# Seven block products in place of eight in the second input projection of a two-block sequence model

## The chip, the cores and the metric

The program runs on one core of one Trainium2 chip, as one launch. Time is the device time of that core in microseconds; the median of three runs counts, and another execution was taken by the hardware profiler.

The engines are named as in the profile: PE (TensorE, matrix multiply; PEld is its weight load), DVE (VectorE), ACT (ScalarE), POOL (GpSimd) and SP (SyncE), which here issues all the DMAs. SPq rows are DMAs being issued by SP.

## The reference

Two blocks follow each other on x of 2048 tokens by 1024. The first is a hybrid of five mixers. The second begins with one large projection, splits its 3784 columns among two mixers, and ends with an output projection and a layer norm:

```python
D_IN_PROJ = int(sum(n for _, n in _SPLITS))
SPLIT_POINTS = tuple(int(v) for v in np.cumsum([n for _, n in _SPLITS])[:-1])
...
        x = _layer_norm(DEEPNORM_ALPHA * x + y, ln_g[layer], ln_b[layer])
    return x
```

The change is about that projection alone: `proj2 = x2 @ w_in_2`, [2048 x 1024] by [1024 x 3784] in float32, where x2 is the first block's output. `proj2` lies in DRAM and is read by the stage behind it.

## The kernel before

The program is a chain of steps. A step (`step`, L127) is a block in which each engine has its own instruction stream, tied by semaphores; it ends when all engines are through, and SP's stream ends by waiting until the step's stores have landed. The second projection (`second_projection`, L221) is one such step, between the last part of the first block (names `fox_`) and the second block's mixers (`ds_`). In the profile its tensors carry the prefix `g_`, but for `second_raw`, the raw weights, which the step before has already loaded with the first column group.

**Precision.** A float32 matmul is made of three matmuls on rounded operands: both sides are split into hi (ACT rounds) and lo (DVE subtracts hi from the original), and hi*hi, hi*lo and lo*hi are summed in PSUM (L301, L302, L303).

**Tiling.** P = 128, KD = 8 slices of the inner dimension, TILES = 16 tiles of 128 rows. The columns are cut into eight groups, seven of 512 and one of 200 (`spans`). The loop is: for each group, for each row tile, 8 k by 3 matmuls into one PSUM bank of four. In the first group PE also turns the tiles of x: `turn(t + 1)` stands ahead of tile t's products, eight transposes from `xt` into `tp`, from which ACT makes `hT.hi` and DVE `hT.lo`. hT stays in SBUF for all groups.

**Weights.** SP loads the next group's weights slice by slice once tile 1 of a group is stored; ACT and DVE split them during the last tile of a group, slice by slice as PE gives them free.

**Results.** ACT copies even tiles and DVE odd tiles out of PSUM into one of four `stage` slots, and SP stores them, 128 x 512 at a time.

Within each engine the order is written out by hand; there is no scheduler. SP's stream is a single one: a DMA behind a wait is not issued until the wait is over.

## Time and profile before

| | |
|---|---|
| median of 3 runs | 4982.17 us (4981.24 to 5010.14) |
| the profiled execution, time | 4980.74 us |
| its span, first to last instruction | 4979.1 us |
| PE busy | 4215.4 us (85%) |
| DVE, ACT, POOL busy | 53%, 39%, 15% |
| granted TensorE clock, mean | 0.865 |
| DMA | 585.32 MB, mean 118 GB/s |
| this projection's first and last matmul | 2541.6 and 3221.5 us |

The page cuts the span into 40 slices of 124.5 us and gives a busy share in tenths for each, and the granted clock in tenths of full speed. Matmuls overlap, so that their busy times can't be added up to a duration: the distance between starts is their price. GB/s counts each moved byte once.

### The profile page before, as it was taken

Reading aid. Unit: us, or ns where it says so; the run is one execution under the profiler, and the core shown is the slowest. Engines: PE = TensorE matmul, PEld = TensorE weight load, DVE = VectorE, ACT = ScalarE, POOL = GpSimd, SP = SyncE. Lnnn points to the kernel's source line nnn. Section 1 sums busy time; section 2 is a strip of 40 time slices with the busy share of each in tenths; the row PEclk is TensorE's granted clock in tenths of the full one; section 3 lists DMA queues with packets and bytes.
Section 4 is the critical chain, followed back from the end, with each engine's and each line's share of the span. In section 5 each row is a group of like instructions: output and inputs, shape, how many; then the busy total and the mean of one; then the engine's idle time right before and its main releaser. Section 6 shows DMA issues by size and latency. Waiting matters only on the chain. (4 is left out here: it accounts for less than half of the span.)

```text
span 4979.1 us, 66174 instructions
## 1 busy us (share of the span) xinstructions
PE 4215.4 (85%) x23522; PEld 3122.5 (63%) x23522; DVE 2660.2 (53%) x5590; ACT 1936.3 (39%) x4022; POOL 735.7 (15%) x755
## 2 busy tenths in 40 slices
PE   7997998985688898889889999877888787877589
PEld 5885777775566666666668888833444444544467
DVE  3113444444666555555421111178889888888546
ACT  3112232323333333333311101035677767767721
POOL 3111111110100000000000000022223333434500
PEclk9998999996589898989899999966578887788789
DMA  5326666664466555545452212210000001010033
GB/s 181 125 113 221 208 214 212 213 216 145 154 206 205 192 188 167 175 159 162 126 178 85 83 66 72 63 52 19 20 20 20 20 20 39 20 39 18 32 140 114
DMA packets 293737, 585.32 MB, mean 118 GB/s; under 512 B 47944, under 2 KB 80364, under 8 KB 293244
## 3 DMA queue, kind: packets, MB, share of 16 engines
q1 hardware_dynamic: 293408, 581.10, 34.7%
q8 instruction: 187, 3.06, 0.2%
q14 instruction: 142, 1.16, 0.1%
HBM read 453.03 MB, written 127.94 MB: 117 GB/s over the span
## 5 line engine op out<-in xcount | busy, mean ns | idle before, releaser
L3059 PE MATMUL ds_big<-ds_ikT,ds_iqT 64*128 64x512 f32 (+3 forms) x608 | 383.2, 761 | 73.6 <-ACT ds_iqT L3036 53.9
L3526 POOL TENSOR_TENSOR ds_E<-ds_bT 128x256 f32<-128x256 f32 x112 | 72.1, 644 | 2380.9 <-ACT ds_bT L3495 2206.1
L301 PE MATMUL g_acc<-g_ws_hi,g_hT_hi 128*128 128x512 f32 (+1 forms) x1024 | 386.2, 377 | 0.0
L302 PE MATMUL g_acc<-g_ws_lo,g_hT_hi 128*128 128x512 f32 (+1 forms) x1024 | 384.6, 376 | 0.0
L303 PE MATMUL g_acc<-g_ws_hi,g_hT_lo 128*128 128x512 f32 (+1 forms) x1024 | 384.6, 376 | 0.0
L529 PE MATMUL mm_big<-mm_gw_hi,mm_ghT_hi 128*128 128x512 f32 (+1 forms) x768 | 319.8, 416 | 30.3 <-PEq L134 30.3
L3115 DVE TENSOR_SCALAR_CACHE_REDUCE ds_seen<-ds_eq,ds_num 128x2048 uint16<-128x2048 uint16 (+13 forms) x224 | 331.3, 1479 | 26.1 <-issue 4.2
L531 PE MATMUL mm_big<-mm_gw_hi,mm_ghT_lo 128*128 128x512 f32 (+1 forms) x768 | 301.4, 392 | 0.0
L530 PE MATMUL mm_big<-mm_gw_lo,mm_ghT_hi 128*128 128x512 f32 (+1 forms) x768 | 300.5, 391 | 0.0
L3155 ACT ACTIVATE ds_signs<-ds_lo,ds_at 128x2048 bf16<-128x2048 uint16 (+13 forms) x224 | 291.3, 1301 | 2.1 <-issue 0.7
L328 DVE COPY g_stage<-g_acc 128x512 f32<-128x512 f32 (+1 forms) x64 | 41.5, 649 | 459.2 <-PE g_acc L303 459.2
L3022 DVE SCALAR_TENSOR_TENSOR ds_score<-ds_rel,ds_iw,ds_score 128x512 f32<-128x512 f32 (+3 forms) x266 | 219.5, 829 | 54.9 <-ACT ds_rel L3043 37.8
L3059 PEld LDWEIGHTS ds_big<-ds_ikT,ds_iqT 64*128 64x128 f32 x608 | 108.2, 235 | 209.7 <-issue 84.1
L347 ACT ACTIVATE g_stage<-g_acc 128x512 f32<-128x512 f32 (+1 forms) x64 | 36.2, 565 | 502.4 <-PE g_acc L303 502.4
L3043 ACT ACTIVATE ds_rel<-ds_big 128x512 f32<-128x512 f32 (+3 forms) x304 | 162.5, 538 | 158.5 <-PE ds_big L3059 85.2
L3634 PEld LDWEIGHTS ds_big<-ds_E 128*128 128x128 f32 x896 | 134.4, 229 | 135.5 <-POOL ds_E L3533 72.6
L303 PEld LDWEIGHTS g_acc<-g_ws_hi,g_hT_lo 128*128 128x128 f32 x1024 | 193.3, 189 | 35.3
L302 PEld LDWEIGHTS g_acc<-g_ws_lo,g_hT_hi 128*128 128x128 f32 x1024 | 193.5, 189 | 34.8
L301 PEld LDWEIGHTS g_acc<-g_ws_hi,g_hT_hi 128*128 128x128 f32 x1024 | 193.5, 189 | 34.6
L3407 PE MATMUL ds_big<-ds_pT,ds_ct 128*128 128x128 f32 x1088 | 169.3, 300 | 53.7 <-ACT ds_pT L3317 53.5
L1635 ACT ACTIVATE fox_pT<-fox_big 128x512 f32<-128x512 f32 (+3 forms) x160 | 85.4, 533 | 323.3 <-PE fox_big L1703 323.1
L1031 PE MATMUL fp_acc<-fp_ws_hi,fp_hT_hi 128*128 128x512 f32 (+1 forms) x528 | 199.2, 377 | 8.8 <-issue 3.6
(550 smaller groups left out, 10083.1 us busy)
## 6 DMA issues: line engine op xcount, KB each, us to landing
fox_ow<-halves SPq DMA_DIRECT2D x600, 256.0 KB, 3.5
mm_ghT_hi<-turned SPq DMA_DIRECT2D x96, 512.0 KB, 4.0
mm_ghT_lo<-turned SPq DMA_DIRECT2D x96, 512.0 KB, 5.3
proj<-g_stage SPq DMA_DIRECT2D x112, 256.0 KB, 2.0
proj<-mm_gstage SPq DMA_DIRECT2D x80, 256.0 KB, 5.0
mm_x<-proj SPq DMA_DIRECT2D x64, 256.0 KB, 3.8
second_raw<-in_w_in SPq DMA_DIRECT2D x56, 256.0 KB, 4.0
proj<-fp_stage SPq DMA_DIRECT2D x48, 256.0 KB, 2.0
```

The costliest lines, as they stand in the source:

```text
L301: pe.matmul(sums, hT.hi[:, k, tile], wt.hi[:, k, 0:width], start=(k == 0), stop=False)
L302: pe.matmul(sums, hT.hi[:, k, tile], wt.lo[:, k, 0:width], start=False, stop=False)
L303: mm = pe.matmul(sums, hT.lo[:, k, tile], wt.hi[:, k, 0:width], start=False, stop=(k == KD - 1))
L529: pe.matmul(sums, b.hT.hi[:, u % 3, k], wt.hi[:, k, 0:width], start=(k == 0), stop=False)
L530: pe.matmul(sums, b.hT.hi[:, u % 3, k], wt.lo[:, k, 0:width], start=False, stop=False)
L531: m = pe.matmul(sums, b.hT.lo[:, u % 3, k], wt.hi[:, k, 0:width], start=False, stop=(k == KD - 1))
L1031: pe.matmul(sums, hT.hi[:, j % 3, n], ws.hi[:, n, at], start=(n == 0), stop=False)
L3022: d = dve.scalar_tensor_tensor(out=score[:, x:x + wd], in0=rel[:, n % 2, 0:wd], scalar=sg, in1=score[:, x:x + wd], op0=ALU.mult, op1=ALU.add)
L3059: pe.matmul(big[:, n % 2, 0:wd], iqT[o, h // 2], b.ikT[o, x:x + wd], start=True, stop=True)\
L3115: dve.tensor_scalar(seen, hi, cand, 0.0, ALU.is_ge, ALU.add, accum_out=count)
L3155: act.activation(signs, lo, ACT.Sign, bias=now, accum_out=sums[:, bit:bit + 1])
L3407: m = pe.matmul(big[:, 5, h * P:(h + 1) * P], b.ct[:, x // P + t], pT[:, (h * NP + p) % 2, t], start=(p == 0 and t == 0), stop=(x + (t + 1 ...
```

## The change

The columns 512 to 1223 (`SIDE`, 712 wide) are multiplied as before. The other 3072 are taken as three pairs of groups of 512 (`PAIRS`), and each pair is computed by the seven products of Strassen and not by eight. The unit is a quadrant: of x, a row tile (of two neighbouring tiles) by half of the inner dimension; of the weights, half of the inner dimension by one group of the pair. Seven combinations of x (five sums or differences, and two quadrants as they are) meet seven combinations of the weights, and each product is added to one or two of the four results.

The step is now two steps.

*First block* (`turned_and_side`): PE turns two tiles at a time, and ACT and DVE split them into `aT`. From the same PSUM banks ACT keeps two quadrants (`kept`), DVE makes five sums (`total`), and these are split too (`S`). SP stores all seven, hi and lo, 0.5 MB each, in the DRAM tensor `combos`: 8 row pairs x 7. PE meanwhile does the side columns, 24 matmuls of 512 and 24 of 200 for a tile. `raw2` holds the 200 columns' weights, whose load is the step's own. The weights of the first two products are loaded on the way, and the first of them is summed and split.

*Second block* (`seven_products`): 168 items, in the order pair, product, row pair. SP streams the combination of each item back from `combos` into one of sixteen slots (`A`). PE does 4 k x 3 matmuls of 512 columns into one bank of eight. ACT copies a first contribution from PSUM into `C`, DVE adds or subtracts the later ones, and SP stores a result when its last is in. For the weights SP loads one or two quadrants (`quad_loads`), POOL adds them (`quad_sum`), and ACT and DVE split the sum, two blocks, one block ahead.

PE, the last products of the first block and the first of the second, after the change (`g_wd` are the side weights, `g_A` a slot of combinations, `g_b` the split weight sums):

```order
7387 L375 MATMUL g_acc<-g_wd_hi,g_aT 128x512
7388 L375 MATMUL g_acc<-g_wd_hi,g_aT 128x200
7389 L377 MATMUL g_acc<-g_wd_lo,g_aT 128x512
7390 L377 MATMUL g_acc<-g_wd_lo,g_aT 128x200
7391 L379 MATMUL g_acc<-g_wd_hi,g_aT 128x512
7392 L379 MATMUL g_acc<-g_wd_hi,g_aT 128x200
7393 L134 UNCONDITIONAL_BRANCH
7394 L545 UNCONDITIONAL_BRANCH
7395 L561 MATMUL g_acc<-g_b_hi,g_A 128x512
7396 L562 MATMUL g_acc<-g_b_lo,g_A 128x512
7397 L563 MATMUL g_acc<-g_b_hi,g_A 128x512
```

Where one run of matmuls stood, a step's end now lies between two.

SP, two column groups of the projection before (`g_stage` are results, `second_raw` the next group's weights):

```order
1071 L247 DMA second_raw<-in_w_in 128x512 x8
1072 L265 DMA proj<-g_stage 128x512 x16
1073 L247 DMA second_raw<-in_w_in 128x512 x8
1074 L265 DMA proj<-g_stage 128x512 x16
1075 L247 DMA second_raw<-in_w_in 128x512 x8
```

The sixteen stores of a group and eight weight loads are all that it issued in 87 us of the trace. SP after the change, from the start of the second block into the fourth product, the first that completes results (`g_C`):

```order
1083 L515 DMA g_A<-combos 128x1024 x21
1084 L246 DMA second_raw<-in_w_in 128x4x512 x2
1085 L515 DMA g_A<-combos 128x1024 x8
1086 L246 DMA second_raw<-in_w_in 128x4x512
1087 L515 DMA g_A<-combos 128x1024 x8
1088 L246 DMA second_raw<-in_w_in 128x4x512
1089 L515 DMA g_A<-combos 128x1024 x5
1090 L523 DMA proj<-g_C 128x512
1091 L515 DMA g_A<-combos 128x1024
1092 L523 DMA proj<-g_C 128x512
1093 L515 DMA g_A<-combos 128x1024
1094 L523 DMA proj<-g_C 128x512
```

Each item now has a load of 0.5 MB, and the weights come as quadrants of 1 MB.

The diff, without the removed body (it stands above) and without the buffers, waits and copies that the words above cover:

```diff
@@ second_projection @@
-def second_projection(nc, c, x, w, out, groups, raw):
...
+SIDE = (512, 712)
+PAIRS = [(0, 1224), (1736, 2248), (2760, 3272)]
+RPS = TILES // 2
+QUAD = KD // 2
+A_SUMS = [((0, 0), (1, 1), ALU.add), ((1, 0), (1, 1), ALU.add), ((0, 1), (0, 0), ALU.add), ((1, 0), (0, 0), ALU.subtract),
+          ((0, 1), (1, 1), ALU.subtract)]
+PURE = [((0, 0), 5), ((1, 1), 6)]
+SEVEN = [(0, (0, 0), (1, 1), ALU.add, ("11", "22"), ()),
+         (4, (1, 0), (1, 1), ALU.add, (), (("11", ALU.add),)),
+         (6, (1, 0), (0, 0), ALU.subtract, ("21",), (("11", ALU.add),)),
+         (2, (1, 1), None, None, ("12",), (("11", ALU.subtract),)),
+         (1, (0, 0), None, None, (), (("21", ALU.add), ("22", ALU.subtract))),
+         (5, (0, 1), (1, 1), ALU.subtract, (), (("12", ALU.add), ("22", ALU.add))),
+         (3, (0, 0), (0, 1), ALU.add, (), (("22", ALU.add),))]
+LAST = {"11": 3, "21": 4, "12": 5, "22": 6}
+PLACE = {"11": 0, "12": 1, "21": 2, "22": 3}
+A_SLOTS = 16
+def quad_loads(sp, raw, w_v, b, arrived):
+    p, m = b // 7, b % 7
+    _, one, two, _, _, _ = SEVEN[m]
+    for a, part in enumerate((one, two)):
+        if part is not None:
+            k0, n0 = part[0] * QUAD, PAIRS[p][part[1]]
+            sp.dma_start(raw[:, a * QUAD:(a + 1) * QUAD], w_v[:, k0:k0 + QUAD, n0:n0 + 512]).then_inc(arrived, 16)
...
+def quad_sum(pool, raw, tmp, b, k, done):
+    _, _, two, op, _, _ = SEVEN[b % 7]
+    if two is None:
+        pool.tensor_copy(tmp[:, k], raw[:, k]).then_inc(done, 1)
+    else:
+        pool.tensor_tensor(tmp[:, k], raw[:, k], raw[:, QUAD + k], op).then_inc(done, 1)
+def second_projection(nc, c, x, w, out, combos, raw):
...
+        bt = [Split(held, f"b{n}", [P, QUAD, 512]) for n in range(2)]
+        tmp = held.sb("tmp", [P, QUAD, 512])
+        with ExitStack() as inner:
+            turned_and_side(nc, c, Buffers(nc, inner, "g2"), x, w_v, out, combos, raw, bt[0], tmp)
+        with ExitStack() as inner:
+            seven_products(nc, Buffers(nc, inner, "g3"), w_v, out, combos, raw, bt, tmp)
...
+def turned_and_side(nc, c, B, x, w_v, out, combos, raw, b0, tmp):
...
+    xt = B.sb("xt", [P, 3, D_MODEL])
+    aT = B.sb("aT", [P, 2, 2, 2, 2, 512], F32R)
+    kept = B.sb("kept", [P, 2, 512])
+    total = B.sb("total", [P, 5, 512])
+    S = B.sb("S", [P, 5, 2, 512], F32R)
+    stage = B.sb("stage", [P, 2, width])
+    tp = B.ps("tp", [P, 2, 2, 512])
+    acc = B.ps("acc", [P, 2, 2, 512])
...
+            rows(0)
+            sp.dma_start(raw2[:], w_v[:, :, c0 + 512:c0 + width]).then_inc(s.raw2_in, 16)
+            rows(1)
+            rows(2)
+            for r in range(RPS):
+                sp.wait_ge(s.a_lo, 4 * (r + 1))
+                for (tile, half), slot in PURE:
+                    sp.dma_start(combos[r, slot], aT[:, r % 2, tile, half].bitcast(F32)).then_inc(a_stored[r % 2], 16)
+                for t in range(2 * r + 3, min(2 * r + 5, TILES)):
+                    rows(t)
+                for i in range(5):
+                    sp.wait_ge(s.s_lo, 5 * r + i + 1)
+                    sp.dma_start(combos[r, i], S[:, i].bitcast(F32)).then_inc(s_stored[i], 16)
+                if r:
+                    results(r - 1)
+                if r == 1:
+                    sp.wait_ge(s.w_lo, KD)
+                    quad_loads(sp, raw, w_v, 0, s.quad_in)
+                if r == 4:
+                    sp.wait_ge(s.b_lo, QUAD)
+                    quad_loads(sp, raw, w_v, 1, s.quad_in)
...
+            def turn(r):
+                for i in range(2):
+                    t = 2 * r + i
+                    pe.wait_ge(x_in[t % 3], 16 * (t // 3 + 1))
+                    if r and i == 0:
+                        pe.wait_ge(s.a_lo, 4 * r)
+                        pe.wait_ge(s.total, 5 * r)
                     for k in range(KD):
...
+                        m = pe.transpose(tp[:, i, k // QUAD, k % QUAD * P:(k % QUAD + 1) * P],
+                                         xt[:, t % 3, k * P:(k + 1) * P], c.ident)
+                    m.then_inc(s.turned, 1)
+            turn(0)
+            for r in range(RPS):
+                for i in range(2):
+                    pe.wait_ge(s.a_lo, 4 * r + 2 * i + 2)
+                    if r:
+                        pe.wait_ge(s.act_out, 2 * (r - 1) + i + 1)
+                        pe.wait_ge(s.dve_out, 2 * (r - 1) + i + 1)
                     for k in range(KD):
...
+                        if r == 0 and i == 0:
+                            pe.wait_ge(s.w_lo, k + 1)
+                        at = slice(k % QUAD * P, (k % QUAD + 1) * P)
+                        hi, lo = (aT[:, r % 2, i, k // QUAD, a, at] for a in range(2))
+                        for n, (u, v) in enumerate(((0, 512), (512, width))):
+                            pe.matmul(acc[:, i, n, 0:v - u], hi, wd.hi[:, k, u:v], start=(k == 0), stop=False)
+                        for n, (u, v) in enumerate(((0, 512), (512, width))):
+                            pe.matmul(acc[:, i, n, 0:v - u], hi, wd.lo[:, k, u:v], start=False, stop=False)
+                        for n, (u, v) in enumerate(((0, 512), (512, width))):
+                            m = pe.matmul(acc[:, i, n, 0:v - u], lo, wd.hi[:, k, u:v], start=False, stop=(k == KD - 1))
+                    m.then_inc(s.product, 1)
+                    if i == 0 and r + 1 < RPS:
+                        turn(r + 1)
...
+                if k == 0:
+                    act.wait_ge(s.raw2_in, 16)
+                act.activation(wd.hi[:, k, 0:512], raw[:, k], ACT.Copy)
+                act.activation(wd.hi[:, k, 512:width], raw2[:, k], ACT.Copy).then_inc(s.w_hi, 1)
+                if k == 2:
+                    a_hi(act, 0, 0)
...
+        def sums_lo(dve, r):
+            dve.wait_ge(s.kept, 2 * r + 2)
+            for n, (one, two, op) in enumerate(A_SUMS):
+                copy = kept[:, 0] if two == (0, 0) else kept[:, 1]
+                dve.tensor_tensor(total[:, n], tp[:, one[0], one[1]], copy, op).then_inc(s.total, 1)
+            for n in range(5):
+                dve.wait_ge(s.s_hi, 5 * r + n + 1)
+                dve.tensor_tensor(S[:, n, 1], total[:, n], S[:, n, 0].bitcast(F32), ALU.subtract).then_inc(s.s_lo, 1)
...
+def seven_products(nc, B, w_v, out, combos, raw, bt, tmp):
...
+    C = B.sb("C", [P, RPS, 4, 512])
+    A = B.sb("A", [P, A_SLOTS, 2, 512], F32R)
+    acc = B.ps("acc", [P, 8, 512])
+    items = [(p, m, r) for p in range(len(PAIRS)) for m in range(7) for r in range(RPS)]
...
+            def weights(q):
+                p, m, r = items[q]
+                sp.dma_start(A[:, q % A_SLOTS].bitcast(F32), combos[r, SEVEN[m][0]]).then_inc(a_in[q % A_SLOTS], 16)
+            def results(q):
+                p, m, r = items[q]
+                for where, last in LAST.items():
+                    if last == m:
+                        tile, n0 = 2 * r + PLACE[where] // 2, PAIRS[p][PLACE[where] % 2]
+                        sp.wait_ge(s.dve_done, dve_by(q))
+                        sp.dma_start(out[tile * P:(tile + 1) * P, n0:n0 + 512], C[:, r, PLACE[where]])\
+                          .then_inc(whole.get(where, stored22[r]), 16)
+            for q in range(A_SLOTS):
+                weights(q)
+            for q in range(N + 2):
+                if q and q - 1 + A_SLOTS < N:
+                    sp.wait_ge(s.product, q)
+                    weights(q - 1 + A_SLOTS)
+                if q >= 2:
+                    results(q - 2)
+                b = q // RPS
+                if q % RPS == 5 and b + 2 < NB:
+                    sp.wait_ge(s.b_lo, QUAD * (b + 1))
+                    quad_loads(sp, raw, w_v, b + 2, s.quad_in)
...
+        @block.tensor
+        def _(pe):
+            for q, (p, m, r) in enumerate(items):
+                b = q // RPS
+                pe.wait_ge(a_in[q % A_SLOTS], 16 * (q // A_SLOTS + 1))
+                if q >= 8:
+                    if acts[q - 8]:
+                        pe.wait_ge(s.act_done, act_by(q - 8))
+                    if dves[q - 8]:
+                        pe.wait_ge(s.dve_done, dve_by(q - 8))
+                bank, slot, right = acc[:, q % 8], A[:, q % A_SLOTS], bt[b % 2]
+                for k in range(QUAD):
+                    if r == 0 and b:
+                        pe.wait_ge(s.b_lo, QUAD * (b - 1) + k + 1)
+                    at = slice(k * P, (k + 1) * P)
+                    pe.matmul(bank, slot[:, 0, at], right.hi[:, k], start=(k == 0), stop=False)
+                    pe.matmul(bank, slot[:, 0, at], right.lo[:, k], start=False, stop=False)
+                    mm = pe.matmul(bank, slot[:, 1, at], right.hi[:, k], start=False, stop=(k == QUAD - 1))
+                mm.then_inc(s.product, 1)
...
+                if b > 1:
+                    pool.wait_ge(s.quad_in, 16 * (quads_in(b + 1) - quads_in(2)))
+                    pool.wait_ge(s.b_lo, QUAD * (b - 1))
+                for k in range(QUAD):
+                    quad_sum(pool, raw, tmp, b, k, s.quad_sum)
...
+                for where in SEVEN[m][4]:
+                    act.wait_ge(s.product, q + 1)
+                    if p and where == "22":
+                        act.wait_ge(stored22[r], 16 * p)
+                    elif p and r == 0:
+                        act.wait_ge(whole[where], 16 * RPS * p)
+                    act.activation(C[:, r, PLACE[where]], acc[:, q % 8], ACT.Copy).then_inc(s.act_done, 1)
+                if r < QUAD and b + 1 < NB:
+                    if b and r == 0:
+                        act.wait_ge(s.product, RPS * b)
+                    act.wait_ge(s.quad_sum, QUAD * b + r + 1)
+                    act.activation(bt[(b + 1) % 2].hi[:, r], tmp[:, r], ACT.Copy).then_inc(s.b_hi, 1)
...
+                if SEVEN[m][5]:
+                    dve.wait_ge(s.product, q + 1)
+                    if m == 1:
+                        dve.wait_ge(s.act_done, act_by(RPS * 7 * p + r))
+                    elif m in (2, 3):
+                        dve.wait_ge(s.act_done, act_by(q))
+                    dve.drain()
+                for where, op in SEVEN[m][5]:
+                    place = C[:, r, PLACE[where]]
+                    dve.tensor_tensor(place, place, acc[:, q % 8], op).then_inc(s.dve_done, 1)
+                if 0 < r <= QUAD and b + 1 < NB:
+                    k = r - 1
+                    dve.wait_ge(s.b_hi, QUAD * b + k + 1)
+                    dve.tensor_tensor(bt[(b + 1) % 2].lo[:, k], tmp[:, k], bt[(b + 1) % 2].hi[:, k].bitcast(F32),
+                                      ALU.subtract).then_inc(s.b_lo, 1)
...
-                            sp.dma_start(raw[:, j], w['w_in_2'][j * P:(j + 1) * P, 0:512]).then_inc(s.raw_in, 16)
+                            sp.dma_start(raw[:, j], w['w_in_2'][j * P:(j + 1) * P, SIDE[0]:SIDE[0] + 512]).then_inc(s.raw_in, 16)
...
+    combos = nc.dram_tensor("combos", [TILES // 2, 7, P, 2, 512], F32, kind="Internal").ap()
...
-            second_projection(nc, c, x2, w['w_in_2'], proj2, spans((0, COLS2)), raw)
+            second_projection(nc, c, x2, w['w_in_2'], proj2, combos, raw)
```

## Rows read from the trace of the kernel before

**Rows 1.** The page: busy time, share and count; PE's busy tenths in 40 slices.

```profile
PE 4215.4 (85%) x23522; PEld 3122.5 (63%) x23522; DVE 2660.2 (53%) x5590; ACT 1936.3 (39%) x4022; POOL 735.7 (15%) x755
...
PE   7997998985688898889889999877888787877589
```

**Rows 2.** Windows: stretch, its us, busy us by engine, granted clock, DMA share, GB/s.

```profile
2700.00:3100.00 400.00, 400.00 (x1766) 331.24 (x1765) 52.10 (x77) 47.42 (x77) 0.00 (x0) 1.00 0.19 70
```

**Rows 3.** Groups by shape in the projection: busy us, mean ns, idle before.

```profile
L301 PE MATMUL g_acc<-g_ws_hi,g_hT_hi 128*128 128x512 f32 x896 | 351.2, 392 | 0.0
...
L354 DVE TENSOR_TENSOR g_ws_lo<-second_raw,g_ws_hi 128x512 fp32r<-128x512 f32 x50 | 33.7, 692 | 35.5 <-ACT g_ws_hi L341 35.5
...
L341 ACT ACTIVATE g_ws_hi<-second_raw 128x512 fp32r<-128x512 f32 x48 | 30.4, 634 | 2.5
L320 DVE TENSOR_TENSOR g_hT_lo<-g_tp,g_hT_hi 128x512 fp32r<-128x512 f32 x30 | 19.6, 687 | 77.4 <-ACT g_hT_hi L313 77.4
...
L341 ACT ACTIVATE g_ws_hi<-second_raw 128x200 fp32r<-128x200 f32 x8 | 3.0, 371 | 2.2 <-PE g_acc L303 2.1
L354 DVE TENSOR_TENSOR g_ws_lo<-second_raw,g_ws_hi 128x200 fp32r<-128x200 f32 x8 | 2.9, 367 | 8.0 <-ACT g_ws_hi L341 8.0
```

**Rows 4.** Timeline of SP: start us, us, what; weight loads of two column groups.

```profile
2668.63 3.79 SPq L247 DMA_DIRECT2D second_raw<-in_w_in  x8
...
2755.67 3.78 SPq L247 DMA_DIRECT2D second_raw<-in_w_in  x8
```

**Rows 5.** Timeline, the projection's end and the next step's first DMA.

```profile
3221.45 0.27 PE L303 MATMUL g_acc<-g_ws_hi,g_hT_lo 128*128 128x200 f32 x1
...
3222.16 0.32 SPq L265 DMA_DIRECT2D proj<-g_stage  x1
...
3224.55 1.86 SPq L3678 DMA_DIRECT2D ds_score<-proj  x2
```

**Rows 6.** Timeline, the projection's start.

```profile
2538.05 8.71 SPq L254 DMA_DIRECT2D g_xt<-x  x7
...
2541.58 1.97 PE L283 MATMUL g_tp<-consts_sb,g_xt 128*128 128x128 f32 x8 [7.63 <-DMA g_xt<-x]
...
2546.07 0.78 PE L301 MATMUL g_acc<-g_ws_hi,g_hT_hi 128*128 128x512 f32 x1
```

**Rows 7.** Timeline of PE, after a late tile of x.

```profile
2578.87 1.12 PE L283 MATMUL g_tp<-consts_sb,g_xt 128*128 128x128 f32 x4 [6.49 <-DMA g_xt<-x]
...
2580.21 0.63 PE L302 MATMUL g_acc<-g_ws_lo,g_hT_hi 128*128 128x512 f32 x1
2580.64 0.63 PE L303 MATMUL g_acc<-g_ws_hi,g_hT_lo 128*128 128x512 f32 x1
...
2582.67 0.40 PE L302 MATMUL g_acc<-g_ws_lo,g_hT_hi 128*128 128x512 f32 x1
```

**Rows 8.** DMA issues of the whole run: count, KB each, median us to landing.

```profile
mm_ghT_hi<-turned SPq DMA_DIRECT2D x96, 512.0 KB, 4.0
...
ds_ct<-proj SPq DMA_DIRECT2D x1, 1024.0 KB, 8.6
```

**Rows 9.** Windows of earlier stages, columns as in rows 2.

```profile
400.00:440.00 40.00, 22.82 (x95) 18.71 (x96) 11.51 (x15) 10.55 (x19) 11.79 (x8) 0.73 0.81 275
...
420.00:430.00 10.00, 10.00 (x43) 8.12 (x42) 3.70 (x7) 0.74 (x2) 0.94 (x1) 0.90 0.99 357
...
620.00:630.00 10.00, 8.18 (x41) 6.10 (x40) 7.24 (x13) 2.73 (x6) 5.01 (x4) 1.00 1.01 370
2500.00:2530.00 30.00, 25.05 (x91) 15.27 (x90) 1.28 (x2) 0.00 (x0) 0.00 (x0) 1.00 0.84 271
```

**Rows 10.** Timeline of PE inside the window 420 to 430.

```profile
427.66 0.39 PE L531 MATMUL mm_big<-mm_gw_hi,mm_ghT_lo 128*128 128x512 f32 x1
427.88 0.39 PE L529 MATMUL mm_big<-mm_gw_hi,mm_ghT_hi 128*128 128x512 f32 x1
```

**Rows 11.** Groups by shape of POOL: an addition of 128 x 512.

```profile
L3283 POOL TENSOR_TENSOR ds_L<-ds_sel,ds_bias 128x512 f32<-128x512 f32 x52 | 67.1, 1301 | 116.4 <-PE ds_big L3400 76.2 <-POOLq L134 40.2
```

More of the change, by code:

```diff
@@ new lines, with quads_in @@
+LAST = {"11": 3, "21": 4, "12": 5, "22": 6}
[8 more added lines that the diff above has]
+            sp.dma_start(raw[:, a * QUAD:(a + 1) * QUAD], w_v[:, k0:k0 + QUAD, n0:n0 + 512]).then_inc(arrived, 16)
+def quads_in(b):
+    return sum(1 + (SEVEN[i % 7][2] is not None) for i in range(b))
@@ L225, in second_projection @@
+def quad_sum(pool, raw, tmp, b, k, done):
[5 more added lines that the diff above has]
+def second_projection(nc, c, x, w, out, combos, raw):
     w_v = w.rearrange("(k p) n -> p k n", p=P)
+    c0, width = SIDE
+    rest = width - 512
     with ExitStack() as ctx:
-        B = Buffers(nc, ctx, "g2")
-        hT = Split(B, "hT", [P, KD, SEQ])
@@ L370 @@
 class Named:
     pass
-def spans(*ranges):
-    return [(n, min(512, b - n)) for a, b in ranges for n in range(a, b, 512)]
 UNITS = 6
```

257 lines of the change are left out of this document (138 added, 119 removed).

## Prediction

> **What bounds the kernel now.** I read the page first (share and slices of each engine), then the stretches of this projection, its groups by shape, its timeline at start and end, and last the DMA rows of other stages, since the change leans on the DMA engines.
>
> The page shows that this is a long program of stages [rows 1]; the projection is the run of nines in PE's slices. In its middle TensorE is busy for 400.00 of 400.00 us at full clock while VectorE and ScalarE work an eighth of the time and the DMA engines 0.19 [rows 2]. So nothing but matmuls bounds it. One column group of 512 goes by in 2755.67 - 2668.63 = 87.04 us [rows 4]; it holds 16 x 8 x 3 = 384 matmuls, so a matmul of 512 columns advances the stage by 0.2267 us (the 392 ns of its group [rows 3] are busy time of overlapping instructions, not a price). The step runs from 2538.05 [rows 6] to 3221.56, the last matmul's start plus one pitch of 0.11 [rows 5]: 683.5 us. Of these 7 x 87.04 + 384 x 0.11 = 652 are products and some 14 are 128 transposes; the other **17.5 us** are start, a late tile of x (TensorE waits 6.49 us [rows 7]) and matmuls at the lower clock.
>
> **Matmuls removed.** Before: 7 x 384 = 2688 matmuls of 512 columns and 384 of 200. After: 384 of 512 and 384 of 200 in the first block, then 3 pairs x 7 x 8 row pairs x 4 x 3 = 2016 of 512, in all 2400 and 384. 288 fewer x 0.2267 = **-65.3 us**. The transposes stay 128. The pitch already includes the sixteen waits of a group; the waits that an item of twelve now has are met ahead, if the data is there.
>
> **Start of the first block.** Now ScalarE must have raw2, 0.82 MB in 800-byte rows, before it splits the first weights. The nearest rows: the first load of a step lands after 2541.58 - 2538.05 = 3.5 us [rows 6], a 1 MB load of 512-byte rows after 8.6 [rows 8]; I take 5.0, so 2543.1. Each k then costs ScalarE 0.634 + 0.371 and VectorE 0.692 + 0.367 = 1.06 us [rows 3]. VectorE's third k is at 2547.2, two tile subtractions of 0.687 later (2548.6) the first product may start, against 2546.07 before [rows 6]. It takes 24 x (0.2267 + 0.11) = 8.1 us and about 1.4 more at the lower clock, to 2558.1; the remaining weights (2553.9) don't hold it. Then TensorE must turn the next two tiles, which now waits for all five sums of the first pair, because they are read from the same banks: VectorE's last tile subtractions end at 2555.3, a copy of 0.6 and five sums of 0.69 end at 2559.4. Tile 3 of x is asked for behind two stores at 2556.2 and takes 4.0 [rows 8] to 5.3 us. So TensorE resumes at about 2561.5, and pays 1.4 us of lower clock again: the row at half speed advances 0.43 us per matmul, and after a wait of 6.49 us that lasted from its restart at 2578.87 to before 2582.67, some 3 us of matmuls, of which half is lost [rows 7]. Counted the same way as the 17.5 of before, this is about 14: **-3.5 us**.
>
> **Rounds of the first block.** A round is 2 x 8.1 + 1.7 = 17.9 us of TensorE. VectorE has 14 x 0.69 + 2 x 0.37 = 10.4 us in it, ScalarE 13 x 0.6 = 7.8. The chain turn, round, subtract, copy, five sums ends about 8.3 us after the turn and is wanted 17.9 after it; the first halves are wanted after 9.8 and ready after 4.2. SP stores 7 x 0.52 MB and two results of 0.36 MB and loads 1.05 MB: 5.4 MB, 303 GB/s. A result's store stands behind the five sums' stores, so ScalarE may find its stage slot late by 1 to 3 us, inside the 5.6 of slack. In rounds 1 and 4 the quarters of a later block's weights add 2.1 MB each. I charge **+2 us**; bounds 0 and 21 (3 us in each of seven rounds).
>
> **The new step boundary.** From the last matmul 3221.56 to the next step's first DMA 3224.55 are 3.0 us [rows 5]; the first of sixteen loads of 0.52 MB lands 4.0 us later [rows 8], and the lower clock costs 1.4: **+8.4 us**. The last sums end in an addition of 0.69 where a 200-column copy of 0.37 stood: **+0.3**.
>
> **The seven products.** An item is 12 matmuls, 2.72 us; a block is 8 items, 21.8 us. Work beside it: VectorE at most 16 additions and 4 subtractions, 14 us; ScalarE at most 16 copies and 4 roundings, 12 us; GpSimd 4 sums of 1.30 us [rows 11]. All fit, and eight banks of sums give 19 us of slack. What is new is DMA: per pair 56 row sums of 0.524 MB, 12 quarters of 1.05 MB and 32 results of 0.262 MB make 50.3 MB in 152.3 us, **331 GB/s**, in blocks 4 to 7 of a pair even 8.4 MB in 21.8 us, 386 GB/s. In full 10 us windows the engines, wholly busy, moved 357 and 370 GB/s [rows 9]. At 357 a heavy block needs 23.5 us, 1.7 too many, four in a row 7; the sixteen slots of row sums hold 40 us of TensorE's work and refill in the three lighter blocks. So I charge nothing; if this cover went, each missing us would be a us of TensorE. Nor does heavy DMA slow the matmuls: inside the 357 GB/s window they follow each other in 0.22 us [rows 10]. The whole step moves 88.1 + 33.6 + 25.2 = 147 MB in 457 us.
>
> The Trainium skill speaks against this: its page DMA: Bandwidth & Descriptors, section Bandwidth, asks for transfers of at least 1 MiB to get 75% of a peak that it puts at 436 GB/s. Our row sums are half that size, so by it they would stay under 327 GB/s, and a pair would last 50.3 / 0.327 = 154 us, at least 5 us more over three pairs. The trace does not agree: its transfers of 256 and 512 KB, queued one behind another, give the 357 and 370 above. It may still be right for the mix with stores, and the rivals below hold that case by rows.
>
> **The sum.** -65.3 - 3.5 + 2 + 8.4 + 0.3 = -58.1. Against the profiled execution, 4980.74 us, this gives 4922.6; the median of the three runs lies 1.4 higher, so I forecast **4924 us** for it.
>
> **Rivals.**
> - *DMA paces the products a little.* For it: the busiest stretch of 40 us that I read holds 275 GB/s, and at the end of the stage before TensorE waits for loads at 271 [rows 9]. Against: those stages ask for no more, or hold only five slots of 256 KB in flight. Between 321 and 284 GB/s the step lasts 457 to 517 us: 4924 to 4982, no change at the far end.
> - *DMA paces it below 284 GB/s: slower than before.* The place is TensorE's wait for a row sum slot, the price 147 MB / rate - 457 us, and break-even where that is 58, at 284 GB/s. At 275 it is 78 us: 5002; at 250, 131 us: 5055; the lower clock after each wait adds to it. It would need reads, stores and strided weight rows together to run a quarter below the 370.
> - *The chain of the first block doesn't fit its round*, for instance because stores hold back ScalarE's copy. Three to four us in seven rounds: 21 to 28, 4943 to 4950.
> - *The products don't keep the pitch:* an item's waits cost TensorE a bubble though met. At 0.1 us for 168 items 17 us: 4941. The pitch across the tile boundaries of before shows none [rows 4].
>
> **How the numbers follow.** Forecast (within 9 us of 4924) 0.64; first block or bubbles 0.14 (4933 to 4950); DMA a little 0.13 (4933 to 4982); DMA slower than before 0.07; better than 4915 is 0.02. The range leaves out the better end, and of the two DMA cases what lies above 4954 (some 0.14): **4914 to 4954**. About 1%, 50 us, is what a measurement of this kernel can tell; the forecast is 58 below, only 8 us clear of that line at 4932. Faster by over 1%: the forecast's 0.64 less the part above 4932, plus the 0.02: 0.62. Slower by over 1% (above 5032, under 259 GB/s): 0.05. Within: 0.33.
>
> **What would show it.** Two stretches of nines for TensorE, about 150 and 457 us, with a gap of 7 us between them; clock 1.00 in the second; items 2.72 us apart to the end; DMA about 320 to 330 GB/s there and its share 0.85 to 0.95; TensorE's waits for a row sum slot only at the step's start. The first block right: one wait of about 3 us at its second turn, none later. Wrong: TensorE waiting for DMA in blocks 5 to 7 of a pair (rate), for the turned tiles in later rounds (chain), or a pitch above 0.227 with no wait named (bubbles).

## The result, and the profile after

| | before | after |
|---|---|---|
| median of 4 runs each | 4983.25 us | 4926.17 us |
| all runs | 4981.24 to 5010.14 | 4908.25 to 4938.61 |
| ratio, 95% interval | | 0.9879 [0.9845, 0.9912] |
| the profiled execution | 4980.74 us | 4908.25 us |
| this projection, first DMA to the next stage's first DMA | 686.5 us | 632.4 us |

57.1 us less, forecast 58.1. The last line is the one that the change can be judged by. It runs from 2538.05 to 3224.55 before [rows 5, 6] and from 2521.86 to 3154.25 after: 54.1 us less. The two profiled executions differ by 72.5 us, because the unchanged stages ahead of the projection happened to end 16.2 us earlier in the second and those behind it took 2.2 us less. In the traces below these earlier stages end anywhere between 2522 and 2550 us with the same code. In what follows the two steps are measured by themselves. The second lasts 466.2 to 467.1 us in every trace below whose edit leaves its pace alone. The first is less steady: with its code unchanged it lasts 164.5 to 167.9 us in eight traces. In the table of experiments the medians take in all executions, and the ratios leave out those in which the clock granted to TensorE was far lower (one of the repeat, 5113 us, and two of the kernel before beside it, 5492 and 6593 us).

The page of the changed kernel, the rows that answer to [rows 1]: busy time, PE's busy tenths, and what the DMA engines moved in each of 40 slices.

```profile
PE 4134.1 (84%) x23234; PEld 3056.9 (62%) x23234; DVE 2827.3 (58%) x5850; ACT 2012.1 (41%) x4162; POOL 833.5 (17%) x839
...
PE   7996999986688898989879999877888877877579
...
GB/s 185 122 112 220 199 220 212 220 201 165 171 186 206 192 205 179 176 161 149 135 253 295 345 317 335 210 37 20 20 20 20 20 22 38 20 39 22 30 145 112
```

288 matmuls fewer, and DMA at 295 to 345 GB/s where [rows 2] had 70.

The start of the first step, answering to [rows 6] (timeline; in brackets the engine's idle time before the row and what ended it):

```profile
2521.86 0.33 SPq L306 DMA_DIRECT2D g_xt<-x  x1
...
2527.86 0.63 ACT L413 ACTIVATE g_wd_hi<-second_raw 128x512 fp32r<-128x512 f32 x1 [51.45 <-DMA g_raw<-in_w_in]
...
2532.76 0.96 PE L375 MATMUL g_acc<-g_wd_hi,g_aT 128*128 128x512 f32 x2 [1.63 <-DVE g_aT L445]
2533.52 0.84 PE L377 MATMUL g_acc<-g_wd_lo,g_aT 128*128 128x512 f32 x2
...
2539.06 0.51 PE L377 MATMUL g_acc<-g_wd_lo,g_aT 128*128 128x512 f32 x2
2539.40 0.51 PE L379 MATMUL g_acc<-g_wd_hi,g_aT 128*128 128x512 f32 x2
...
2545.46 1.09 PE L357 MATMUL g_tp<-consts_sb,g_xt 128*128 128x128 f32 x8 [0.54 <-DMA g_xt<-x]
```

The 200-column weights let ScalarE start 6.0 us into the step. The first product follows at +10.90. A pair of matmuls (512 and 200 columns) takes 0.64 us at first and 0.34 from the fourth slice on: nine pairs at the lower clock (granted 0.50 from 2532.76 to 2538.64, that is 1.2 GHz).

The first step's rounds. The turn of two tiles, x16, starts a round. Then come two products that wait, the first with the rows that release it:

```profile
2581.15 1.91 PE L357 MATMUL g_tp<-consts_sb,g_xt 128*128 128x128 f32 x16
...
2599.41 1.91 PE L357 MATMUL g_tp<-consts_sb,g_xt 128*128 128x128 f32 x16
...
2626.66 0.60 ACT L426 ACTIVATE g_stage<-g_acc 128x512 f32<-128x512 f32 x1 [11.07 <-DMA proj<-g_stage]
...
2627.15 2.06 ACT L391 ACTIVATE g_aT<-g_tp 128x512 fp32r<-128x512 f32 x4
...
2629.12 0.59 PE L375 MATMUL g_acc<-g_wd_hi,g_aT 128*128 128x512 f32 x2 [1.08 <-DVE g_aT L445]
...
2637.46 1.91 PE L357 MATMUL g_tp<-consts_sb,g_xt 128*128 128x128 f32 x16
2649.13 0.59 PE L375 MATMUL g_acc<-g_wd_hi,g_aT 128*128 128x512 f32 x2 [1.52 <-DVE g_aT L445]
2657.47 1.91 PE L357 MATMUL g_tp<-consts_sb,g_xt 128*128 128x128 f32 x16
```

The undisturbed round is 2599.41 - 2581.15 = 18.26 us. The one that begins at 2637.46 and holds the second wait takes 2657.47 - 2637.46 = 20.01, the one before it, with the first wait, 19.57. Read backwards, TensorE waits for VectorE's halves of the turned tiles, these for ScalarE's, and ScalarE had stood 11.07 us before its copy, because the stage slot was still being stored.

The boundary between the steps and the end, answering to [rows 5]:

```profile
2683.64 0.50 PE L379 MATMUL g_acc<-g_wd_hi,g_aT 128*128 128x512 f32 x2
...
2684.81 0.32 SPq L313 DMA_DIRECT2D proj<-g_stage  x1
2687.81 9.81 SPq L515 DMA_DIRECT2D g_A<-combos  x16
2691.03 0.80 PE L561 MATMUL g_acc<-g_b_hi,g_A 128*128 128x512 f32 x1 [6.88 <-DMA g_A<-combos]
2691.62 0.63 PE L562 MATMUL g_acc<-g_b_lo,g_A 128*128 128x512 f32 x1
...
2695.86 0.39 PE L563 MATMUL g_acc<-g_b_hi,g_A 128*128 128x512 f32 x1
...
3150.14 0.39 PE L563 MATMUL g_acc<-g_b_hi,g_A 128*128 128x512 f32 x1
...
3154.25 1.71 SPq L3921 DMA_DIRECT2D ds_score<-proj  x2
```

From 2683.98 to 2691.03, 7.05 us without a product; then 459.3 us to 3150.37; then 3.9 us to the next stage.

The products by stretches (us, busy us by engine PE, PEld, DVE, ACT, POOL, granted clock, DMA share, GB/s). The first row is the whole second step, the others single blocks of eight items, 21.76 us each: a light one, then the fifth to seventh of the first pair, which ask for the most data.

```profile
2684.00:3151.00 467.00, 459.64 (x2018) 380.05 (x2016) 186.57 (x273) 102.01 (x177) 90.69 (x80) 0.99 0.87 315
...
2734.55:2756.31 21.76, 21.76 (x98) 18.02 (x97) 7.82 (x12) 5.81 (x11) 2.29 (x4) 1.00 0.77 266
2778.07:2799.83 21.76, 21.76 (x98) 18.02 (x97) 11.82 (x19) 3.58 (x6) 5.59 (x4) 1.00 1.03 388
2799.83:2821.59 21.76, 21.76 (x98) 18.02 (x97) 13.54 (x21) 2.54 (x4) 5.51 (x4) 1.00 1.03 388
2821.59:2843.35 21.76, 21.76 (x98) 18.02 (x97) 10.29 (x15) 2.54 (x4) 5.50 (x4) 1.00 1.02 392
```

TensorE is busy for 21.76 of 21.76 us whether the engines move 266 or 392 GB/s; from the first wait of 6.88 us to the end no wait of PE is recorded. The forecast asked of the heavy blocks 386 GB/s and bounded the engines' rate by the 370 of [rows 9]: they gave 388 to 392.

### The profile page after: what moved, and what is told of

Its sections match the earlier page's. It is cut to its first block and busy times, and to the rows that moved or that the text cites. A ratio compares the mean times of both kernels' runs of the same rounds, so it can differ in the third digit from the quotient of the medians.

```text
span 4906.6 us, 66655 instructions
## 1 busy us (share of the span) xinstructions
PE 4134.1 (84%) x23234; PEld 3056.9 (62%) x23234; DVE 2827.3 (58%) x5850; ACT 2012.1 (41%) x4162; POOL 833.5 (17%) x839
## 5 line engine op out<-in xcount | busy, mean ns | idle before, releaser
L259 POOL TENSOR_TENSOR g_tmp<-second_raw 128x512 f32<-128x512 f32 x60 | 83.4, 1421 | 1578.8 <-DMA second_raw<-in_w_in 1470.8
L561 PE MATMUL g_acc<-g_b_hi,g_A 128*128 128x512 f32 x672 | 262.5, 391 | 6.9 <-DMA g_A<-combos 6.9
L610 DVE TENSOR_TENSOR g_C<-g_C,g_acc 128x512 f32<-128x512 f32 x192 | 127.6, 685 | 237.9 <-PE g_acc L563 152.1
L562 PE MATMUL g_acc<-g_b_lo,g_A 128*128 128x512 f32 x672 | 262.3, 390 | 0.0
L563 PE MATMUL g_acc<-g_b_hi,g_A 128*128 128x512 f32 x672 | 262.1, 390 | 0.0
L3265 DVE SCALAR_TENSOR_TENSOR ds_score<-ds_rel,ds_iw,ds_score 128x512 f32<-128x512 f32 (+3 forms) x266 | 217.0, 819 | 56.3 <-ACT ds_rel L3286 40.2
L3877 PE MATMUL ds_big<-ds_E 128*128 128x128 f32 x896 | 155.3, 327 | 60.0 <-POOL ds_E L3776 39.5
L3650 PEld LDWEIGHTS ds_big<-ds_pT,ds_ct 128*128 128x128 f32 x1088 | 143.1, 203 | 87.8 <-ACT ds_pT L3560 75.9
L1276 PE MATMUL fp_acc<-fp_ws_hi,fp_hT_lo 128*128 128x512 f32 (+1 forms) x528 | 196.0, 371 | 0.0
L1275 PE MATMUL fp_acc<-fp_ws_lo,fp_hT_hi 128*128 128x512 f32 (+1 forms) x528 | 195.1, 369 | 0.0
```

What stands on the lines that cost most here:

```text
L561: pe.matmul(bank, slot[:, 0, at], right.hi[:, k], start=(k == 0), stop=False)
L562: pe.matmul(bank, slot[:, 0, at], right.lo[:, k], start=False, stop=False)
L563: mm = pe.matmul(bank, slot[:, 1, at], right.hi[:, k], start=False, stop=(k == QUAD - 1))
L3265: d = dve.scalar_tensor_tensor(out=score[:, x:x + wd], in0=rel[:, n % 2, 0:wd], scalar=sg, in1=score[:, x:x + wd], op0=ALU.mult, op1=ALU.add)
L3650: m = pe.matmul(big[:, 5, h * P:(h + 1) * P], b.ct[:, x // P + t], pT[:, (h * NP + p) % 2, t], start=(p == 0 and t == 0), stop=(x + (t + 1 ...
L3877: m = pe.matmul(big[:, 6 + l % 2, h * P:(h + 1) * P], E[:, l % 2, h], E[:, l % 2, h], start=True, stop=True)
```

## The experiments

Each kernel is the changed one with one edit. "First" is the time from the first step's first DMA to the second's, "second" from there to the next stage's; ratios are against the kernel before, run on the same chip.

| kernel | first | second | median | ratio |
|---|---|---|---|---|
| the changed kernel | 165.95 | 466.4 | 4926.17 | 0.9879 [0.9845, 0.9912] |
| again, unchanged | 166.5 | 466.4 | 4917.64 | 0.9879 [0.9847, 0.9912] |
| no loads of combinations | 166.5 | 467.0 | 4931.48 | 0.9911 [0.9875, 0.9946] |
| extra loads for each item | 167.9 | 482.2 | 4943.63 | 0.9922 [0.9899, 0.9946] |
| extra loads for every second item | 164.5 | 466.3 | 4938.64 (one run) | |
| four slots | 165.9 | 506.7 | 4969.34 | 0.9965 [0.9941, 0.999] |
| two matmuls for three | 165.7 | 389.1 | 4847.99 | 0.9724 [0.97, 0.9748] |
| loads in two halves | 167.2 | 467.1 | 4932.21 | 0.9892 [0.9871, 0.9912] |
| both edits of the first step | 159.4 | 466.2 | 4927.11 | 0.9877 [0.9859, 0.9895] |
| side weights early | 159.0 | 466.9 | 4922.33 (one run) | |
| results sooner | 162.8 | 466.7 | 4927.00 (one run) | |

**Again.** No edit.

> The changed kernel once more, to read its spread and a second trace. Theory (the two new steps are paced by TensorE and alike in every run): the projection's two steps last 632 us within 3 us again, the products 457 to 460 us, and what differs between runs lies in the steps ahead of them, whose code is unchanged; median 4915 to 4940. Rival (the spread of 4908 to 4939 us comes from the new DMA load): the projection's length differs between the two traces by 10 us or more.

The second step repeats to 0.01 us and the first to 0.54; the ratio is the same.

**No loads.** Leaves out the reload of row combinations: after the sixteenth item the products run on what lies in the slots.

```diff
-                if q and q - 1 + A_SLOTS < N:
-                    sp.wait_ge(s.product, q)
-                    weights(q - 1 + A_SLOTS)
...
-                pe.wait_ge(a_in[q % A_SLOTS], 16 * (q // A_SLOTS + 1))
+                if q < A_SLOTS:
+                    pe.wait_ge(a_in[q % A_SLOTS], 16)
```

> Leaves out the loads of row combinations after the first sixteen, so that later products reuse what lies in the slots (the output is not the reference's); all matmuls, weight loads and stores stay. Theory (TensorE's matmuls pace the second step, DMA is hidden): no change, its products last 457 to 460 us at 59 MB in place of 147, total within 15 us of the changed kernel. Rival (the DMA load costs time that no wait shows, in slower matmuls or in the spread): products shorter by 10 us or more, or a spread as narrow as that of the kernel before.

Its window of the products, columns as above:

```profile
2720.00:3150.00 430.00, 430.00 (x1899) 356.18 (x1898) 180.04 (x264) 92.49 (x160) 80.31 (x76) 1.00 0.39 133
```

133 GB/s in place of some 320, and 467.0 us in place of 466.4. The 152 loads that it leaves out, 80 of the 88 MB of streaming, cost nothing that this can measure, and neither do their waits where they are met. (The step still moved 67 MB; the expectation had 59.)

**Two matmuls for three.** Leaves out the product of the lo part of x, so that TensorE needs a third less time for the same DMA.

```diff
                     pe.matmul(bank, slot[:, 0, at], right.hi[:, k], start=(k == 0), stop=False)
-                    pe.matmul(bank, slot[:, 0, at], right.lo[:, k], start=False, stop=False)
-                    mm = pe.matmul(bank, slot[:, 1, at], right.hi[:, k], start=False, stop=(k == QUAD - 1))
+                    mm = pe.matmul(bank, slot[:, 0, at], right.lo[:, k], start=False, stop=(k == QUAD - 1))
```

> Leaves out the third matmul (lo by hi) of every k in the seven products, so that an item has 8 matmuls in place of 12 (the output lacks that term); all DMAs, sums and copies stay. TensorE alone would need 1344 x 0.2267 = 305 us for the second step's products in place of 457, DMA 147 MB at the 390 GB/s of the heaviest blocks 377. Theory (DMA is the next bound, 80 us below TensorE's): the second step, 466 us in three traces, lasts 380 to 400, TensorE waiting for row combinations. Rival (no bound but TensorE down to there): 315. Rival (the queue cannot hold such a rate over the whole step, 340 or less): 440 or more.

TensorE's waits in its products (us in total, times, longest), the stretch, and GB/s in 40 slices of it:

```profile
PE g_acc L561 <- DVE g_b_lo L613: 42.2, 34, 5.8
```

```profile
2711.00:3050.00 339.00, 301.12 (x1199) 235.64 (x1199) 172.95 (x243) 89.33 (x161) 82.51 (x72) 0.92 1.02 396
```

```profile
GB/s 411 403 402 311 413 400 407 395 409 404 403 410 397 406 403 404 405 401 336 414 372 398 400 410 403 400 409 397 408 399 405 404 403 334 411 359 380 403 408 399
```

The matmuls would need 1344 x 0.2267 = 305 us; the engines need 146.9 MB / 0.396 = 371. The step lasts 389.1, of which 381.8 lie between the first product and the last. The 11 us above 371 belong to the step's end, where little is left to move: its last three of 40 slices show 208, 181 and 135 GB/s. Seen from TensorE, the 381.8 are 305 of matmuls at their pitch, 42.3 of waits and 34.3 that matmuls at the lower clock took longer. So DMA is the next bound, at 396 GB/s. It shows not as a wait for row combinations, as was expected, but for the weights' sum (`g_b_lo`): the quadrants of 1 MB stand in the same queue as everything else, and a block cannot begin without them, while the slots hold sixteen items. POOL, which adds the quadrants, waits for their landing for 255.7 of the 339 us.

**Extra loads.** Twelve slots to make room, and for each item one more load of 0.26 MB that nobody uses; in a weaker form for every second item.

```diff
-A_SLOTS = 16
+A_SLOTS = 12
...
+                    if q > 8:
+                        sp.wait_ge(spare_in[(q - 1) % 8], 16 * ((q - 1) // 8))
+                    sp.dma_start(spare[:, (q - 1) % 8], combos[q % RPS, 0, :, 0]).then_inc(spare_in[(q - 1) % 8], 16)
```

> Adds a load of 0.26 MB per item into spare slots (156 of them), with twelve slots for the row combinations in place of sixteen: 188 MB in place of 147 in the second step, 411 GB/s if it kept TensorE's pace. Theory (the sixteen DMA engines end near the 394 GB/s that they moved in blocks with share 1.03, and the step then becomes theirs): 188 MB / 394 = 477 us and a few us at the lower clock, so 18 to 35 us longer, TensorE waiting for row combinations in blocks 4 to 7 of a pair. Rival (there is more room than that): products still 460 us. Rival (the mix with stores falls to 340 GB/s once queues are full): 550 us, 90 longer.

> As the run with extra loads, but one load of 0.26 MB at every second item (78 of them, twelve slots): 167 MB, 366 GB/s at TensorE's pace, 434 in the four heavy blocks of a pair. Theory (an average below the ceiling of some 394 is enough, since twelve slots carry 30 us over a heavy stretch that falls 9 us behind): second step 466 to 470 us. Rival (what counts is the heavy blocks' own rate): 9 us and more for each pair, 490 or more.

The full form, its stretch and waits:

```profile
2711.00:3050.00 339.00, 331.12 (x1440) 270.70 (x1440) 131.16 (x184) 69.45 (x122) 66.17 (x57) 0.99 1.04 398
```

```profile
PE g_acc L568 <- DVE g_b_lo L621: 7.9, 12, 2.4
```

41 MB more make 188 MB, which at 398 GB/s take 472 us; the products' 457 are exceeded by 15, and the step grew by 15.8, less than the 18 to 35 expected. The waits are again for the weights' sums and not, as expected, for the combinations. The half form adds 20 MB, 167 MB, 420 us: under 457, and the step kept 466.3. Together they bracket where DMA begins to count: between 167 and 188 MB per 457 us, 365 and 411 GB/s of demand, with the rate at 396 to 398 between them. The half form also shows that twelve slots do as well as sixteen, in its one trace.

**Four slots.**

```diff
-A_SLOTS = 16
+A_SLOTS = 4
```

> Four slots for row combinations in place of sixteen, nothing else. Theory (the heavy blocks run the DMA engines at their ceiling and only the 40 us of row combinations ahead hide it; loads there take 7 us and more to land, three items ahead are 8.2 us): TensorE waits in blocks 4 to 7 of each pair, 10 to 40 us in all with the lower clock. Rival (the rate alone counts, and it suffices): products 460 us as before, no change.

```profile
2711.00:3050.00 339.00, 319.64 (x1351) 260.52 (x1352) 119.95 (x184) 69.31 (x120) 56.88 (x54) 0.96 0.87 294
```

```profile
PE g_acc L560 <- DMA g_A<-combos: 31.2, 11, 6.9
```

The bytes are the same, and their mean rate is far below what the engines can do, yet the step is 40.2 us longer. Here is the wait that the change could have had. It comes where two quadrants of 1 MB stand ahead of a combination in SP's stream (SP's timeline of the same kernel; 2.99 us of TensorE's wait end at 2806.51):

```profile
2794.75 0.94 SPq L246 DMA_DIRECT2D second_raw<-in_w_in  x2
2795.73 0.89 SPq L514 DMA_DIRECT2D g_A<-combos  x1
2796.66 1.07 SPq L522 DMA_DIRECT2D proj<-g_C  x1
```

Four slots hold 10.9 us of work, and a 1 MB quadrant alone takes 7.6 us to land there. Over the whole step the waits for slots are 33.4 us where the changed kernel has 6.9, so 26.5 of the 40.2. Another 12.7 are matmuls at the lower clock: 81 of them follow the one before by more than 0.33 us with no wait between, and exceed their pitch by 15.0 us in all, where the changed kernel has 11 and 2.3. About 1 us stays open. So in this run the waits cost half as much again in clock.

**Loads in two halves.** The same bytes as 0.26 MB transfers (TensorE's wait counts both halves; that line isn't shown).

```diff
-                sp.dma_start(A[:, q % A_SLOTS].bitcast(F32), combos[r, SEVEN[m][0]]).then_inc(a_in[q % A_SLOTS], 16)
+                for a in range(2):
+                    sp.dma_start(A[:, q % A_SLOTS, a].bitcast(F32), combos[r, SEVEN[m][0], :, a])\
+                      .then_inc(a_in[q % A_SLOTS], 16)
```

> Each row combination is loaded by two DMAs of 0.26 MB (hi and lo, rows of 2 KB) in place of one of 0.52 MB (rows of 4 KB). Theory (transfers queued one behind another fill the engines whatever their size): second step 466 us within 3, share of the DMA engines up by one or two hundredths. Rival, from the Trainium skill, page DMA: Bandwidth & Descriptors, section Bandwidth (transfers below 1 MiB stay under 75% of its 436 GB/s): halving the size lowers the rate below the 331 GB/s that a pair needs, and the step grows by 10 us or more with waits for row combinations.

```profile
2711.00:3050.00 339.00, 339.00 (x1494) 280.69 (x1494) 136.73 (x195) 82.61 (x144) 70.90 (x60) 1.00 0.95 341
```

TensorE is busy throughout, and single slices of its DMA row reach 402 GB/s. At this demand, with sixteen slots of cover, halving the loads changes nothing that the step shows; a stream of 0.26 MB loads that saturates the engines wasn't tried.

**The first step.** Two edits, together and then each by itself. *Side weights early*: ScalarE and VectorE split the 512-column part and the first tile before they wait for the 200-column part (first diff, ScalarE's half). *Results sooner*: SP stores the first of a row pair's two results ahead of the next sums, the second after them.

```diff
-                if k == 0:
-                    act.wait_ge(s.raw2_in, 16)
-                act.activation(wd.hi[:, k, 0:512], raw[:, k], ACT.Copy)
+                act.activation(wd.hi[:, k, 0:512], raw[:, k], ACT.Copy).then_inc(s.w_hi, 1)
+            a_hi(act, 0, 0)
+            act.wait_ge(s.raw2_in, 16)
+            for k in range(KD):
```

```diff
                 for t in range(2 * r + 3, min(2 * r + 5, TILES)):
                     rows(t)
+                if r:
+                    results(r - 1, (0,))
                 for i in range(5):
...
                 if r:
-                    results(r - 1)
+                    results(r - 1, (1,))
```

> Two edits of the first step: the weights' 512 columns are split before raw2 is waited for, and a row pair's first result is stored ahead of the next pair's five sums. Theory (the late raw2 costs TensorE some 2.5 us at the start, and ScalarE's 11.5 us waits for a stage slot some 3 us in all rounds): the first step, 166 us from its first DMA to the next step's first, lasts 160 to 162; the total falls by as much, 4 to 6 us, hardly more than the runs can tell. Rival (rounds are set by TensorE's matmuls alone): 163 to 164, the start's part only.

> Alone: the 512-column part of the side weights is split before the wait for the 200-column part, and the first two tile halves are split first. The combined edit took 6.5 us off the first of the two steps (165.9 to 159.4 us). If the late side weights are what delays the first tile, this alone gives about -2.7 us (first product some 1.5 to 3 us earlier, step 163 us). Rival: the stores' order gives all of it, and this gives less than 1 us. Nothing changes in the second step, 466.4 us.

> Alone: the store of a row pair's first result goes ahead of the stores of its sums, so that ScalarE finds its stage slot free. ScalarE's waits for that slot should fall from 72 us in sum to a third or less. If these waits lengthen the rounds, the six rounds of 18.3 to 19.0 us fall by 0.5 us each, the first step by about 3.8 us (to 162). Rival: they are slack, the rounds stay at 18.3 and the step within 1 us of 165.9; then the combined edit's gain was all at the start. Second step 466.4 us.

Side weights early, PE's timeline of the start (its step begins at 2541.20), and its only later wait of that kind:

```profile
2550.15 0.94 PE L375 MATMUL g_acc<-g_wd_hi,g_aT 128*128 128x512 f32 x2
2550.89 0.84 PE L377 MATMUL g_acc<-g_wd_lo,g_aT 128*128 128x512 f32 x2
...
2552.57 0.52 PE L377 MATMUL g_acc<-g_wd_lo,g_aT 128*128 128x512 f32 x2
...
2559.46 1.91 PE L357 MATMUL g_tp<-consts_sb,g_xt 128*128 128x128 f32 x16
...
2577.71 1.91 PE L357 MATMUL g_tp<-consts_sb,g_xt 128*128 128x128 f32 x16
```

```profile
PE g_acc L375 <- DVE g_aT L444: 0.4, 1, 0.4
```

The first product starts at +8.95 in place of +10.90, with no wait ahead of it, and only three pairs run at the lower clock in place of nine; the wait for a tile of x goes as well. The third turn stands at +36.51 in place of +41.04, 4.5 us gained; the expectation had 2.7. The other 2.4 of its 6.9 us come from the late rounds, which lost less in this run than in the changed kernel; the edit doesn't touch what makes them late, and these rounds vary from trace to trace. In the half form of extra loads, whose first step is the changed kernel's word for word, the last two turns were

```profile
2666.06 1.91 PE L357 MATMUL g_tp<-consts_sb,g_xt 128*128 128x128 f32 x16
2684.32 1.91 PE L357 MATMUL g_tp<-consts_sb,g_xt 128*128 128x128 f32 x16
```

18.26 us apart, and no product of its rounds waited. Of the eight traces with that code seven lose 3.3 to 4.7 us in the last three rounds and this one nothing. Why they differ stays open.

Results sooner, its waits (of ScalarE for the slot, and of TensorE for the tile halves, which is the one at the start):

```profile
ACT g_stage L428 <- PE g_acc L381: 69.0, 15, 7.7
```

```profile
PE g_acc L377 <- DVE g_aT L447: 1.6, 1, 1.6
```

ScalarE now waits for the product that it is to copy, and never for a store; before, the same list had this:

```profile
ACT g_stage L426 <- DMA proj<-g_stage: 72.1, 7, 11.7
...
PE g_acc L375 <- DVE g_aT L445: 4.2, 3, 1.6
```

The two late waits of 1.08 and 1.52 us are gone, and 3.1 us of the step with them: not the 0.5 us in each round that was expected, but the last rounds alone. One trace couldn't tell this from the spread just named; but in both traces with this order (this one and both edits) every round behind the third turn takes 18.25 or 18.26 us, as in only one of the nine with the old order. Both edits together give 6.5 us, a little more than the 4 to 6 expected and no more than early alone: the first tile of x landed 0.7 us later in that trace (its first turn stands at +4.33, in early at +3.65). In total time none of the three can be told from the changed kernel: 6 us of 4920 are below what these runs resolve.

## Why the prediction was right, point by point

| term | predicted | measured |
|---|---|---|
| matmuls removed | -65.3 | -65.3 |
| start of the first step | -3.5 | -5.0 |
| its rounds | +2 | +6.3 |
| boundary | +8.4 | +9.35 |
| end | +0.3 | +0.9 |
| products paced by DMA | 0 | 0 |
| sum | -58.1 | -53.8 |

**The matmuls** carry the result. The pitch read from a group of the kernel before [rows 4] held in items of twelve: from the twelfth matmul, 2695.86, to the last, 3150.14, are 2004 pitches in 454.28 us, 0.2267 each. The rival of a bubble for each item is refuted: 0.1 us for each would be 17, and 2004 pitches of 0.2267 leave no room for it.

**DMA** was the step on which the forecast could have turned, and its working held. The engines weren't asked for more than they give: 147 MB in 457 us against a rate of 396 to 398 GB/s, shown by two kernels that drive them to it. Both DMA rivals, a rate under 321 and one under 284, are refuted. The forecast took 357 and 370 [rows 9] as the engines' rate and let the slots cover the difference in heavy blocks; neither that lack nor the cover at sixteen was needed, since the rate is higher than any window of before showed, and twelve slots did. But cover as such is needed: four slots cost 40 us. The Trainium skill's rule (DMA: Bandwidth & Descriptors, section Bandwidth: transfers of at least 1 MiB for three quarters of the peak, which by the prediction's estimate would keep half-size ones under 327 GB/s) is against the runs in its consequence: queued streams in which most transfers were of 0.5 or 0.26 MB ran at 388 to 398. The same page (section Where 436 GB/s comes from) lets the DRAM side bind at about 358 GB/s for transfers between DRAM and SBUF, a core's half share of its stack; its section Bandwidth keeps that figure for both cores streaming. The measured 398 over 339 us, with one core at work, is above it.

**The start.** The forecast had the first product at +10.55 and TensorE back at work behind the second turn at +23.45; measured +10.90 and, with the turn's second half, +23.60. In between it was wrong: it charged 1.4 us for the lower clock, then a wait of 3 us for the sums and tile 3 of x, and the lower clock again. Nine pairs ran at 0.64 in place of 0.34, 2.8 us, which made the first tile end 2 us later; the sums were ready by then, the wait shrank to the 0.54 for a tile of x, and no lower clock followed it. How the delay is shared was off, and little else: of the 162.1 us up to the last side product, 132.5 are pairs (384 x 0.345), 3.1 late rounds and some 14 transposes, so that 12.5 are left for the start against 17.5 before: -5.0.

**The rounds** are the mis-sized term. One part is a price: a pair of 512 and 200 columns was put at 0.2267 + 0.11 = 0.337 and takes 12 pairs in 2543.54 - 2539.40 = 4.14 us, 0.345. Over 384 pairs this is 3.2 us. The other is the sentence "ScalarE may find its stage slot late by 1 to 3 us, inside the 5.6 of slack": in the rounds that begin at 2599.41, 2617.89 and 2637.46 ScalarE's copy started 7.7, 8.8 and 9.2 us after the product that it copies, not 1 to 3, and the rounds lost 0.2, 1.3 and 1.8 us; results sooner, without them, is 3.1 us shorter. "One wait at its second turn, none later" was wrong for that reason: the rival "stores hold back ScalarE's copy" came true in two of the rounds, at an eighth of its price. The charge of 2 with bounds 0 to 21 held the 6.3.

**Boundary and end.** 7.05 us of gap against 7.0; the first eleven matmuls took 4.83 us (2691.03 to 2695.86) where eleven pitches are 2.49, so that the lower clock cost 2.3 against 1.4. From the last product to the next stage there are 3.9 us where the forecast had 3.3: an addition and a store must end before the step does, as was counted; the other 0.6 was not looked into.

The measured terms add up to -53.8, and the steps by themselves gave -54.1; the difference is rounding in the pitches and in the 17.5 of before. The sum is no test of its parts, since the start's stands in it for what the others leave of the first 162.1 us. In the prediction's terms the start and the removed matmuls gave 1.5 us more than forecast, the rounds, the boundary and the end 5.9 less. That the medians differ by 57.1, one us from the forecast, is within their interval, some 17 us either way: the forecast's hit of the total is closer than its terms were.

## What to carry to other kernels

Where TensorE has no gap for hundreds of us, fewer matmuls are worth their full pitch, and DRAM may serve as scratch for the operands as long as bytes over time stay below the engines' rate. Take that rate from a kernel that saturates them, not from the busiest window of one that doesn't. Then ask which load in the shared queue has the least cover: it is that one, not the most frequent, that waits first; and look at the seams between steps, where the 7 us without a product cost another 2.3 at the lower clock.

## What the runs showed of the hardware that was not expected

- The DMA engines held 396 and 398 GB/s for 339 us in two different kernels, with loads of 0.5 and 1 MB (in the second also 0.26) and stores of 0.26 MB in one queue.
- TensorE's matmuls kept 0.2267 us beside it: its busy time is whole in windows of 388 to 392 GB/s.
- Matmuls of 512 and 200 columns in turn take 0.345 us a pair where the single pitches of the kernel before add up to 0.338 (0.2267 and, twelve in 1.34 us from 3189.74, 0.112).
- At the start of the first step TensorE's clock rose from 1.2 to 2.4 GHz (granted 0.50, then 0.99) after nine pairs where a wait of 1.63 us lay between transposes and products, and after three pairs where there was none.
- The same earlier code took 2522 to 2550 us up to this projection in eleven traces, and the first step 164.5 to 167.9 in eight, the second 466.2 to 467.1. So a step's own length tells more than the total does, but how much has to be read from repeats for each step: 1 us in the second, over 3 in the first.
